# The second feed-forward products: where the feature sums are made, how many plain chunks go first, and in which order VectorE sums, splits and reads

## The reference, cut to what matters

```
D_FF = 5632
def conv_ffn(x, w_up, conv_w, conv_b, w_down):
    h = x @ w_up                                   # 256 x 11264
    hp = jnp.pad(h, ((0, 0), (1, 1), (0, 0)))
    h = sum(hp[:, j:j + T, :] * conv_w[j] for j in range(3)) + conv_b
    gate, val = jnp.split(h, 2, axis=-1)
    return (jax.nn.silu(gate) * val) @ w_down      # (256 x 5632) @ (5632 x 2048)
x = layer_norm(ALPHA * x + conv_ffn(...), ln2_g[layer], ln2_b[layer])
```

## Time and profile before

| | before |
|---|---|
| median of three runs | 3313.91 us |
| the profiled execution, its own time | 3313.92 us |
| its span (first to last instruction) | 3312.1 us |
| TensorE busy | 3263.7 us, 99% |
| VectorE busy | 2382.8 us, 72% |
| ScalarE busy | 1445.7 us, 44% |
| GpSimd busy | 288.5 us, 9% |
| down0, from its first product to its last | 949.3 to 1200.5 us |
| down1 | 1968.3 to 2218.7 us |

### The profile page before, as it was taken

One profiled execution on the slowest core, in us unless ns is written; L12 is line 12 of the kernel. 1 busy time (PEld: TensorE's weight loads), 2 busy tenths in 40 slices (PEclk: granted clock), 3 DMA queues, 4 the chain that ended last, 5 costly groups with the idle time before them and its releaser, 6 DMA issues.

```text
span 3312.1 us, 40640 instructions
## 1 busy us (share of the span) xinstructions
PE 3263.7 (99%) x17302; PEld 2811.3 (85%) x17302; DVE 2382.8 (72%) x2310; ACT 1445.7 (44%) x1122; POOL 288.5 (9%) x108
## 2 busy tenths in 40 slices
PE   9999999999989999999999998999999999999999
PEld 8888888888877788888888887778888888888887
DVE  6756778888888886768888878878866466554554
ACT  6534443333334445643333334456733343355433
POOL 1300001111120000000111110000011011000000
PEclk9999999999999999999999999999999999999999
DMA  7554445555544555455555554555455545545554
GB/s 269 190 203 177 154 172 188 188 190 190 191 178 178 206 190 187 139 191 191 191 189 188 188 189 161 203 191 191 176 194 197 191 168 176 195 159 178 208 185 152
DMA packets 88306, 616.22 MB, mean 186 GB/s; under 512 B 10304, under 2 KB 11200, under 8 KB 15296
## 3 DMA queue, kind: packets, MB, share of 16 engines
q1 hardware_dynamic: 83232, 592.35, 49.8%
q10 hardware_dynamic: 4896, 21.30, 1.9%
HBM read 607.32 MB, written 2.10 MB: 184 GB/s over the span
## 4 chain that ended last, share of the span: by engine, by line
PE 91%; DVE 5%; DVEq 2%; ACT 1%; POOLq 0%; issue 0%; DMA 0%; POOL 0%; SPq 0%; ACTq 0%
PE acc L406 53%; PE acc L478 6%; PE acc L479 6%; PE acc L480 6%; PE acc L430 5%; PE acc L432 5%; PE acc L431 5%; DVE w_lo L323 1%; DVEq L1065 1%; DVE over L1066 1%; PE acc L2151 0%; PE acc L1771 0%; PE acc L1835 0%; DMA w_raw<-weights_dram 0%; PE acc L2255 0%
## 5 line engine op out<-in xcount | busy, mean ns | idle before, releaser
L323 DVE TENSOR_TENSOR w_lo<-w_raw,w_hi 128x2048 fp32r<-128x2048 f32 x558 | 1354.4, 2431 | 654.4 <-ACT w_hi L319 651.2
L319 ACT ACTIVATE w_hi<-w_raw 128x2048 fp32r<-128x2048 f32 x558 | 1067.0, 1916 | 1469.4 <-PE acc L406 919.8
L406 PE MATMUL acc<-x_hi_lo,w_hi 128*128 128x512 f32 x5184 | 1212.8, 390 | 1.0 <-DVE w_lo L323 0.7
L406 PEld LDWEIGHTS acc<-x_hi_lo,w_hi 128*128 128x128 f32 x5184 | 961.1, 188 | 194.5 <-issue 2.9
L406 PEld LDWEIGHTS acc<-x_hi_lo,w_lo 128*128 128x128 f32 x5184 | 647.8, 191 | 16.8 <-DVE x_hi_lo L669 1.0
L406 PE MATMUL acc<-x_hi_lo,w_lo 128*128 128x256 f32 x5184 | 659.1, 284 | 1.2 <-DVE x_hi_lo L666 0.6
L478 PE MATMUL acc<-w_hi,hidden_hi_lo 128*128 128x512 f32 x672 | 265.3, 395 | 30.6 <-DVE w_lo L323 30.6
L430 PE MATMUL acc<-w_hi,x_hi_lo 128*128 128x512 f32 x736 | 288.1, 391 | 0.0
L432 PE MATMUL acc<-w_hi,x_hi_lo 128*128 128x512 f32 x736 | 286.5, 389 | 0.0
L431 PE MATMUL acc<-w_lo,x_hi_lo 128*128 128x512 f32 x736 | 286.4, 389 | 0.0
L480 PE MATMUL acc<-w_hi,hidden_hi_lo 128*128 128x512 f32 x672 | 263.2, 392 | 0.0
(11 more groups left out here) (291 smaller groups left out, 2582.6 us busy)
## 6 DMA issues: line engine op xcount, KB each, us to landing
w_raw<-weights_dram SPq DMA_DIRECT2D x558, 1024.0 KB, 4.8
over<-rows_dram ACTq DMA_DIRECT2D x9, 1024.0 KB, 7.2
over<-over ACTq DMA_DIRECT2D x20, 128.0 KB, 2.4
u_tiles<-x_dram SPq DMA_DIRECT2D x4, 512.0 KB, 7.9
w_raw<-weights_dram SPq DMA_DIRECT2D x4, 512.0 KB, 6.9
resid<-x_tok_dram ACTq DMA_DIRECT2D x1, 2048.0 KB, 8.3
over<-w_gates_dram ACTq DMA_DIRECT2D x1, 2048.0 KB, 8.3
out_dram<-resid SPq DMA_DIRECT2D x8, 256.0 KB, 2.1
```

What stands on the lines that cost most here:

```text
L319: act.activation(whi[:, n % NHI, :], w_raw(n), ACT.Copy).then_inc(weights_hi, 1)
L323: dve.tensor_tensor(w_lo(n, 0, CHUNK), w_raw(n), whi[:, n % NHI, :].bitcast(F32), ALU.subtract).then_inc(weights_split, 1)
L406: last = pe.matmul(acc[:, 4 * t + f, 0:cols], weights, moving(k, 0, cols), start=(k == 0 and low == low_first), stop=(k == CK * nch - 1 an ...
```

## The change

- A view `mixed32` of the mixed features' buffer, unrounded. `mix(j)` makes the feature sums there: the additions of high and low part in the place of the future high part of pair j, the four kinds in the place of its future low part. `mix_hi` and `mix_lo` read them there. `mix(0)` no longer waits for GpSimd's last group; that wait stands behind split 7, before `group(0, 0)`, which uses `sums`.
- DOWN_LEAD is (8, 4): nine plain chunks stand ahead of the first b11 and five ahead of the first b11 of half 1, and correspondingly fewer at the end of each half. Loads follow the order of the steps.
- The shared banks of half 0 are dealt out differently (b11 and t1 in 6 and 7, t2 and t3 in 4 and 5). TensorE waits for them in two steps: chunk (4, 2) for the reads of b11, t1 and t3, chunk (4, 3) for that of t2.
- In a group the in-place add comes ahead of the split of the second plain chunk; in second groups `take_p1` comes behind that split and `take_r5_r7` between the last two splits.
- Splits 6 and 7 are made around `mix_lo(1)` instead of in the group. The statistics stand apart from `finals`, in half 0 behind one more split; in half 1 `finals` and the statistics stand ahead of split 55.
- ScalarE loads gamma and beta ahead of its last cast.

The diff, with its smaller pieces left out:

```
-DOWN_LEAD = (6, 2)
+DOWN_LEAD = (8, 4)
...
+        (mixed32,), _ = over(X0, [[P, 2, 2, 4, 4, P]])
...
-        SHARED_BANK = ({"b11": 4, "t1": 5, "t2": 6, "t3": 7}, {"b11": 0, "t1": 1, "t2": 2, "t3": 3})
+        SHARED_BANK = ({"b11": 6, "t1": 7, "t2": 4, "t3": 5}, {"b11": 0, "t1": 1, "t2": 2, "t3": 3})
...
-                if i == down_chunk(4, 2):
-                    pe.wait_ge(shared_out, layer + 1)
+                if i in (down_chunk(4, 2), down_chunk(4, 3)):
+                    pe.wait_ge(shared_out, 2 * layer + i - down_chunk(4, 2) + 1)
...
             def mix_hi(j):
                 act.wait_ge(mixed_raw, 2 * layer + j + 1)
-                act.activation(mixed[:, j, 0].rearrange("p a k n -> p (a k n)"), sums[:, 1, :], ACT.Copy)\
-                   .then_inc(mixed_hi, 1)
+                hi, raw32 = (m.rearrange("p a k n -> p (a k n)") for m in (mixed[:, j, 0], mixed32[:, j, 1]))
+                act.activation(hi, raw32, ACT.Copy).then_inc(mixed_hi, 1)
...
-            for i in range(7, NDOWN - 3):
+            for i in range(7, NDOWN - 1):
                 cast(i)
             act.wait_ge(chunk_used, n0 + down_at(1, 1, "t2") + 1)
             load_row(act, row_g[:], 2 * occ, rows_landed)
             load_row(act, row_b[:], 2 * occ + 1, rows_landed)
-            for i in range(NDOWN - 3, NDOWN):
-                cast(i)
+            cast(NDOWN - 1)
...
             def mix(j):
-                pair = DOWN_PAIRS[j]
+                pair, kinds = DOWN_PAIRS[j], mixed32[:, j, 1]
+                both = mixed32[:, j, 0].rearrange("p a k n -> p (a k n)")
+                whole = [both[:, h * CHUNK // 2:(h + 1) * CHUNK // 2].rearrange("p (k n) -> p k n", k=4) for h in range(2)]
...
-                dve.tensor_tensor(lo, sums[:, 1, :], hi.bitcast(F32), ALU.subtract).then_inc(mixed_ready, 1)
+                hi, lo, raw32 = (m.rearrange("p a k n -> p (a k n)") for m in (mixed[:, j, 0], mixed[:, j, 1], mixed32[:, j, 1]))
+                dve.tensor_tensor(lo, raw32, hi.bitcast(F32), ALU.subtract).then_inc(mixed_ready, 1)
...
                 split(i0 + 2)
+                add(i0, held_raw(held, "b12"), held_raw(held, "b12"), held_raw(held, "b22"))
                 split(i0 + 3)
-                add(i0, held_raw(held, "b12"), held_raw(held, "b12"), held_raw(held, "b22"))
+                if j:
+                    take_p1(p)
                 split(i0 + 4)
                 split(i0 + 5)
                 used(down_at(p, j, "t1"))
                 add(i0, t1, t2, held_raw(held, "b21"))
                 split(i0 + 6)
                 split(i0 + 7)
+                split(i0 + 8)
                 if j:
-                    take_p1(p)
-                split(i0 + 8)
+                    o = take_r5_r7(p)
+                    if p == 0:
+                        o.then_inc(shared_out, 1)
                 split(i0 + 9)
...
-            split(3)
-            split(4)
-            dve.wait_ge(hid_ready, (layer + 1) * FG + 1)
+            splits(3, 5)
+            dve.wait_ge(chunk_used, n0)
             mix(0)
             split(5)
-            dve.wait_ge(chunk_used, n0)
             mix_lo(0)
             mix(1)
+            split(6)
             mix_lo(1)
+            split(7)
+            dve.wait_ge(hid_ready, (layer + 1) * FG + 1)
             group(0, 0)
             group(0, 1)
-            take_r5_r7(0)
-            split(26)
+            second = down_at(1, 0, "b11") - 1 - DOWN_LEAD[1]
+            everything = ((0, 0), (1, 0), (0, 1), (1, 1))
+            split(second)
             take_r6(0).then_inc(shared_out, 1)
-            split(27)
-            split(28)
-            split(29)
-            used(27)
-            finals(0, ((0, 0), (1, 0), (0, 1), (1, 1))).then_inc(acc_free, 2)
+            splits(second + 1, second + 3)
+            used(second - 2)
+            finals(0, everything).then_inc(acc_free, 2)
+            split(second + 3)
+            final_stats(0, everything)
             group(1, 0)
             group(1, 1)
-            take_r5_r7(1)
-            split(50)
+            split(NDOWN - 4)
             take_r6(1).then_inc(acc_free, 1)
-            split(51)
-            split(52)
-            split(53)
-            split(54)
+            splits(NDOWN - 3, NDOWN - 1)
             used(down_chunk(10, 2))
             finals(1, ((0, 0), (1, 0)))
-            split(55)
+            final_stats(1, ((0, 0), (1, 0)))
+            split(NDOWN - 1)
```

More of the change, by code:

```diff
@@ L1038, in used @@
                 dve.wait_ge(chunk_used, n0 + i + 1)
-            first_half, second_half = sums[:, 0, 0:CHUNK // 2], sums[:, 0, CHUNK // 2:CHUNK]
-            whole = [a.rearrange("p (k n) -> p k n", k=4) for a in (first_half, second_half)]
-            kinds = sums[:, 1, :].rearrange("p (a k n) -> p a k n", a=4, k=4)
             def mix(j):
-                pair = DOWN_PAIRS[j]
+                pair, kinds = DOWN_PAIRS[j], mixed32[:, j, 1]
+                both = mixed32[:, j, 0].rearrange("p a k n -> p (a k n)")
+                whole = [both[:, h * CHUNK // 2:(h + 1) * CHUNK // 2].rearrange("p (k n) -> p k n", k=4) for h in range(2)]
                 for a, c in zip(whole, pair):
@@ L1060, in mix_lo @@
                 dve.wait_ge(mixed_hi, 2 * layer + j + 1)
-                hi, lo = (mixed[:, j, part].rearrange("p a k n -> p (a k n)") for part in range(2))
-                dve.tensor_tensor(lo, sums[:, 1, :], hi.bitcast(F32), ALU.subtract).then_inc(mixed_ready, 1)
+                hi, lo, raw32 = (m.rearrange("p a k n -> p (a k n)") for m in (mixed[:, j, 0], mixed[:, j, 1], mixed32[:, j, 1]))
+                dve.tensor_tensor(lo, raw32, hi.bitcast(F32), ALU.subtract).then_inc(mixed_ready, 1)
             def add(i, dst, a, b):
@@ L1092, in finals, with final_stats @@
                     o = dve.tensor_tensor(zp, zp, acc[:, FINAL_BANK[p][b][n], :], ALU.add)
+                return o
+            def final_stats(p, places):
                 dve.drain()
@@ L1095, in finals @@
                     dve.bn_stats(stats[:, b, 2 * p + n, :], target(p, b, n))
-                return o
             PLUS, MINUS = ALU.add, ALU.subtract
@@ L1106, in take_r5_r7 @@
                 take(p, "t1", (((0, 1), PLUS), ((1, 1), PLUS)))
-                take(p, "t3", (((1, 0), MINUS), ((1, 1), PLUS)))
+                return take(p, "t3", (((1, 0), MINUS), ((1, 1), PLUS)))
             def take_r6(p):
@@ L1134, in group, with splits @@
                 split(i0 + 7)
+                split(i0 + 8)
                 if j:
-                    take_p1(p)
-                split(i0 + 8)
+                    o = take_r5_r7(p)
+                    if p == 0:
+                        o.then_inc(shared_out, 1)
                 split(i0 + 9)
+            def splits(first, end):
+                for i in range(first, end):
+                    split(i)
             last_value(FG - 1, 1, range(2))
             last_value(FG - 1, 2, range(2, 4))
-            split(3)
-            split(4)
-            dve.wait_ge(hid_ready, (layer + 1) * FG + 1)
+            splits(3, 5)
+            dve.wait_ge(chunk_used, n0)
             mix(0)
             split(5)
-            dve.wait_ge(chunk_used, n0)
             mix_lo(0)
             mix(1)
+            split(6)
             mix_lo(1)
+            split(7)
+            dve.wait_ge(hid_ready, (layer + 1) * FG + 1)
             group(0, 0)
             group(0, 1)
-            take_r5_r7(0)
-            split(26)
+            second = down_at(1, 0, "b11") - 1 - DOWN_LEAD[1]
+            everything = ((0, 0), (1, 0), (0, 1), (1, 1))
+            split(second)
             take_r6(0).then_inc(shared_out, 1)
-            split(27)
-            split(28)
-            split(29)
-            used(27)
-            finals(0, ((0, 0), (1, 0), (0, 1), (1, 1))).then_inc(acc_free, 2)
+            splits(second + 1, second + 3)
[3 more added lines that the diff above has]
+            final_stats(0, everything)
             group(1, 0)
             group(1, 1)
-            take_r5_r7(1)
-            split(50)
+            split(NDOWN - 4)
             take_r6(1).then_inc(acc_free, 1)
-            split(51)
-            split(52)
-            split(53)
-            split(54)
+            splits(NDOWN - 3, NDOWN - 1)
             used(down_chunk(10, 2))
             finals(1, ((0, 0), (1, 0)))
-            split(55)
+            final_stats(1, ((0, 0), (1, 0)))
+            split(NDOWN - 1)
             if name == "down0":
```

## The result

The changed kernel takes 3286.63 us (median of 4 runs, 3286.53 to 3287.54), the kernel before beside it 3314.34 (the three runs of before and a fourth, 3314.76). The ratio is 0.9918 with a 95% interval of 0.9901 to 0.9935: 27.7 us, 0.8% faster. The forecast was 3287.5. On the chip of the last comparison it took 3287.58 against 3313.01, ratio 0.9922 (0.9909 to 0.9936). The profiled execution took 3286.53 us around a span of 3284.7.

What follows compares the result with a forecast made beforehand. TensorE, busy in 99% of the span, bounds the kernel. Losses of 22.4 us (down0) and 21.5 (down1) fall to 8.3 and 9.2, winning 14.1 and 12.3: 3313.9 - 26.4 = 3287.5 us, range 3277 to 3299.

Steps and rivals of the forecast that it cites:

- before step 6, with restart: TensorE idle 3.3 us before step 6 of each down stage, 3.7 us lost with the restart.
- clock: Granted clock falls to half around step 6 in both stages, costing 3.0 us each; bounds 0 and 5.1.
- short waits in groups: None in first groups; 0.15 and 0.6 us late in second groups, 1.6 us per stage with restarts.
- Part 1: Feature sums in their own buffer: mix 0 starts at 965.97, loses 2.4 us to GpSimd, ends at 973.6.
- the cast at nothing: GpSimd's cast beside mix 0 costs VectorE nothing; only the subtraction holds it, for 2.4 us.
- rival B: VectorE does not yield to GpSimd: step 6 starts 2.4 us earlier, no clock fall, 3276.7 us; chance 0.12.
- rival E: Mix 0 still held until 969.6; step 6 starts 1.3 us later, 3290 us; no separate chance.
- Part 2: Split 6 before mix-lo 1, eight chunks in front: step 6 starts at 985.6 instead of 991.13, further front costs hidden.
- Part 3: New order inside groups: no wait in first groups, 1.6 us per stage from second groups, against 10.2 before.
- rival C: Order inside groups does not pay, TensorE keeps the short waits: 3304.7 us, half of it 3296; chance 0.13 with its half.
- D: Moved instructions enter TensorE's path once splits' 0.9 us slack is used up: 39 us cost, 3324 us; chance 0.03.
- Rival A: Clock kept in both stages around step 6: 6.0 us less, 3281.5 us; chance 0.10.

Runs made afterwards that it cites:

- e6: Changed kernel, but GpSimd's last operation of the last group copies instead of subtracting (this changes the low part of the result); 3282.3 us.
- e1: Changed kernel, but mix 0 waits for GpSimd's last group again; 3288.52 us.
- e7: Kernel before, with only the feature sums in the mixed features' buffer and mix 0's wait dropped; 3311.98 us against 3313.76.
- e4: Changed kernel with six instead of eight plain chunks in front of the first group, the two put behind it; 3293.74 us.
- e2: Changed kernel, but in each group the in-place add stands behind the second plain chunk's split again; 3299.06 us.
- e3: Changed kernel, but in second groups the four reads of b11's bank stand behind t4's split again; 3289.84 us.
- e10: Changed kernel with b11's four reads in two pairs and split 55 ahead of the final reads of half 1; 3283.81 us.
- the second profile: Changed kernel itself, unedited, measured and profiled again on the chip of the last comparison; 3287.58 us.
- e5: Changed kernel with 15 idle products of 128 columns issued in TensorE's idle time before step 6; 3283.09 us.
- e8: Changed kernel with split 6 ahead of mix-lo 0, split 7 ahead of mix 1, split 8 ahead of mix-lo 1, casts moved to match; 3280.77 us.

## Why the prediction was right, step by step

The time (3287.5 against 3286.63) and the mechanism both came out; four of its terms were off, partly against each other. Losses per stage, forecast and measured:

| term | forecast | down0 | down1 |
|---|---|---|---|
| before step 6, with restart | 3.7 | 4.35 | 4.3 |
| clock | 3.0 | 1.7 | 1.7 |
| short waits in groups | 1.6 | 1.9 | 1.9 |
| end of down1 | 0.9 | - | 0.76 |
| won against before | 14.1 / 12.3 | 14.6 | 12.9 |

The before-step-6 value is 986.38 - 949.39 less six steps of 5.44; the short waits are what is left of the products from 1007.11 to 1185.64 beyond 779 x 0.2267 us (5.44 / 24). The clock row is of the first profile; the second one has 1.6 and 2.9. That the sum fits so much better than its terms is partly luck: in down0 the clock was put 1.3 us too high, the front and the short waits together 0.95 too low.

**Part 1, the port.** The step "the cast at nothing" failed, by a misread row. The first addition took 2.06 us, 0.9 more than alone, because the cast had its turn before it. The prediction found that the cast beside split 4 took its usual time, 2.83 us; but the usual time is itself one spent waiting. Every cast of the up stages begins while a split runs, as in this pair:

```profile
918.26 3.97 DVE L324 TENSOR_TENSOR w_lo<-w_raw,w_hi 128x2048 fp32r<-128x2048 f32 x1 [0.72 <-ACT w_hi L320]
920.30 2.83 POOL L905 CAST hidden_hi_lo<-over 128x1024 f32 x1 [0.22 <-issue]
```

The split ends at 922.23 and the cast at 923.13, 0.90 later. So it is in all 22 casts of the changed kernel's trace, and in e6 also where a cast begins later within the split (up1: 2.47 us, from 1522.14) or beside an addition (the copy: 1.84): each ends 0.90 us after VectorE's operation. The cast itself therefore takes about 0.9 us (an estimate from these ends; no trace has one alone), and that is what it cost the first addition. The subtraction cost the 2.2 left of 3.1 (forecast 2.4). e6 fits: a cast and a copy of 0.9 each, against 1.7 us of hold. The Trainium skill (SBUF — State Buffer, "SBUF: two separate sides") describes an exclusive lock that the other engine waits for in full; all these rows agree with it, the casts too, and counting the cast at nothing went against it. GpSimd gets in between two VectorE operations that would follow each other at once: rival B is out. So is rival E; e1, which builds it, has its price right (split 6 at 984.48 is 1.3 us behind the forecast's 983.15).

**No wait at step 5.** Right, by 0.1 us: split 5 ended at 976.66.

**Part 2, the front.** Right: split 6 at 983.95 instead of 983.15, 0.7 of it from the port and 0.1 from a later start of the stage. What carried it is not the dropped wait (e1, e7: some 1 us in all) but that split 6 stands ahead of mix-lo 1 (4.2 us earlier per stage, by the two pairs under e7_own), and the two chunks more (e4: 6 to 7 us).

**Part 3, the groups.** Right in its waits, and the largest part. That two splits queue up behind the late add is shown by e2 (12.4 us, theory 12.6), and the order of the reads by e3 and e10. The splits' slack of 0.9 us, worked out from the cast ring, held: no plain chunk or split in a first group was late. Rivals C and D fall. One sum of it is wrong: it counts three adds to a group where `group` has four. With four, VectorE's work is 31.5 us in a first group and 36.7 in a second, against 35.4 of products. So a second group does not fit barely; it overruns by 1.3 us and lives on the lead that VectorE has gained before it. In the first second group of down0 the ten splits with what stands between them last from 1028.36 to 1066.10, 37.7 us with 1.4 of short gaps:

```profile
1028.36 2.29 DVE L324 TENSOR_TENSOR w_lo<-w_raw,w_hi 128x2048 fp32r<-128x2048 f32 x1 [0.42 <-ACT w_hi L320]
...
1066.10 2.29 DVE L324 TENSOR_TENSOR w_lo<-w_raw,w_hi 128x2048 fp32r<-128x2048 f32 x1
```

The waits were carried forward operation by operation, with all four adds, so this sum did not enter the forecast time. It stands under rival C only, whose case it makes too weak.

**The clock.** The mis-sized term: 3.0 against 1.7 in the profile beside the result, though the second profile has 2.9 in one stage. That it falls was right. I took the price from stretches of 10.2 us whose falls came into a long idle time (3.9 and 2.0 us into it by the granted clock, not 3.6 and 1.7); in the first profile it fell after TensorE had resumed and came back after 3.4 us. e5, in which it does not fall, gains 3.5 us for both stages. Where the fall comes varies between runs of one kernel, so part of how far the term was off is chance. Rival A (no fall) would have given 3.4 us less, not 6.0.

**Not tested alone.** No run takes back the lead of half 1 (4 instead of 2), the new dealing of the shared banks with its two waits, the place of `take_r5_r7`, or that of the statistics. The parts that runs take back (e1, e2, e3, e4) add up to 23 to 25 us of 27.7, but nothing shows that they simply add.

## What to carry to other kernels

When a ring of few buffers sits between two engines, work out the slack of each stage of the ring first (here 0.9 us); an operation longer than that in front of a split in a hand-written order can become a wait. Here moving one such operation past one split was worth 12.4 us, and removing a dependency 1. A dropped wait is worth only what the work does in the time gained: look for what else then uses the same port. A wait that vanishes in one place is a debt until the engine has a gap to pay it in; with the casts' gaps in the timeline one can say in which line the gap is.

## What the hardware showed that was not expected

- VectorE's two-operand operations and GpSimd's hold each other to the end, a cast with its one operand included. Casts that began during a VectorE split or addition ended 0.90 us after it, however long they had waited (1.84 to 2.91 us in the trace, e6). So an operation of GpSimd that takes the same time in every group, 2.83 us here, need not be running alone: look at what ends just before it does. A GpSimd subtraction went from 2.45 to 3.15 us behind an addition.
- Between two VectorE additions with nothing between them in the program, the waiting GpSimd operation had its turn (second addition held from 968.1 to 970.48).
- With 3.9 us left idle TensorE's clock fell in every stage of every profile, from 1.8 us before TensorE resumed (e1, down1) to 1.3 us after (the changed kernel, down0), for 3.4 or 6.8 us. In the kernel before it was 10.2. With 2.8 us of idle time (e6) it fell in one stage and not in the other, and with 1.6 (e8) in none.
- 15 products of 128 columns, 3.5 us of them, kept it up (e5).
